# Late bank, early tokens, a gate product in column groups: an edit in four places of a two-block transformer kernel

## The chip, the cores and the metric

The kernel runs on one core of one Trainium2 chip. The metric is the device time of one execution in microseconds, the median of several runs. TensorE does the matmuls, VectorE, ScalarE and GpSimd the rest, and SyncE (SP) issues nearly all loads.

## The reference, cut to what matters

Two transformer blocks of two layers each run over 256 tokens of width 1024, all float32.

```python
for l in range(2):                         # first block
    mod = silu(c) @ w_ada[l] + b_ada[l]    # 6 vectors of 1024: sh1, sc1, g1, sh2, sc2, g2
    h = layer_norm(x) * (1 + sc1) + sh1
    x = layer_norm(ALPHA * x + g1 * mixer(h, w_in[l], ...), ln1[l])   # projections, rope, attention
    h = layer_norm(x) * (1 + sc2) + sh2
    x = layer_norm(ALPHA * x + g2 * moe(h), ln2[l])      # 16 experts of width 256, 2 of them per token
# second block
h = x @ w_in; q, k, v, r, lr = split(h)    # lr has 16 columns
log_a = log_sigmoid(lr @ w_gate2 + b_gate) / 16          # 16 -> 512
# ... gated linear attention, then experts of width 512, then differential attention, experts again
```

There are four expert stages, moe0 to moe3. In each of them a token goes to two of 16 experts; the weights of all 16 are read.

## The kernel before

**The stream.** All large weights come from memory as a stream of 212 slots of 2 MB (128 x 4096), in the order of use. A slot lands in one of several banks of on-chip memory: ring 0 to 3, and up to five more that are open only in some spans of the stream (`OPEN`): two banks at the end of `area` (`RING`, `RING + 1`), one in the constants `cst` (`RING + 2`), one more in `area`, one in `early`. `ring_order` deals out the banks ahead of time: each slot takes the open bank that was given out longest ago, and a bank that has just opened comes first. SP issues the loads strictly in the order of the slots (L1504). Ahead of each load it waits until the slot that last lay in that bank has been used, and ahead of the first load into a bank that has just opened it waits for what lay there: in the expert stages for the last sums of the output projection before them (`acc_filled`). A slot that waits holds back all behind it. Behind slot `kvq` SP issues 16 small loads of the relative bias (`load_rel_bias`, L1490), which wait for the last slot that lay in bank `RING + 1`.

The names of slots: `ada_first` (4 pieces of w_ada), `in0`, `pa0`, `out0`, `moe0` (24 slots), the same for layer 1, `gla_in` (6), `gla_out` (2), `moe2` (48), `v`, `kvq`, `kvq_rest`, `v_rest`, `diff_out`, `moe3` (48).

**The start.** SP issues three small tables, slot 0, slot 1, the tokens X, slot 2, and then the rest. TensorE multiplies each of the four first pieces of w_ada by silu(c) in column groups (`ada_parts`, L904: partial sums in four groups of 32 columns, kept apart), ScalarE copies them out (`ada_take`), and TensorE sums the groups and the partitions by a product with ones (`ada_finish`, L925). ScalarE then makes `mod_col`. VectorE norms the tokens (L2069, L2088), TensorE flips them (`flip_tokens`, L588), and ScalarE writes the flipped and scaled tokens to `HT` (`take_tile`, L1556), for which it needs all four pieces. Then the products with w_in start (L549, L566).

**Other pieces of w_ada.** 20 more are weighed and summed over k by VectorE or GpSimd (`ada`) during the mixer. TensorE sums them over the partitions (`ada_sums`). For gains the result is wanted on all partitions: a product with ones in f32 (L921), and a product of a one-hot column with the table of biases (L922). Two pieces of each layer, 10 and 11 (`ADA_LATE`), are summed in `ada_late`, in the expert stage, right ahead of the counts.

**The expert stages.** VectorE ranks the scores and writes `chosen_h` (L2289). TensorE counts with it each token's place in its expert's queue (L693 to L696). From this VectorE makes `SEL` (`select`, L2383), the matrices that gather the tokens. The tokens are split into a high part `X_HI` and a low part `X_LO` in float32r; ScalarE writes the high parts, GpSimd the low part of the first tile (L510) and VectorE that of the second (`low_part`, L2262). TensorE gathers both parts of both tiles (`gather`, L706), ScalarE and VectorE scale the result to `XG`, and then eight pairs of experts follow: `up` (L749), the activation, `down` (L801), and the scatter to the tokens (L783). `residual_norm` ends the stage.

**The gate of the second block.** TensorE makes lr, transposed, by eight matmuls of 16 columns (`flipped` with n=16), as the input tile `HT` of the second token tile comes from ScalarE. ScalarE copies it to `LRT` (16 rows). For each token tile one product with w_gate2 (16 rows, L1212) and one with the bias (1 row, L1213) follow. While VectorE and ScalarE make the log decay, TensorE works on the next slot (L566).

Of the kernel before, what the change touches and what calls it, by code (L numbers as in the profile page):

```python
# [71 lines left out]
ADA_SPLIT = [4, 5]  # L72

# [46 lines left out]
for _name, _n in (("ada0", W), ("ada1", W), ("gate2", W), ("b_gate", W), ("rel", DH)):  # L120
    ROWS[_name] = (N_ROWS, _n)
    N_ROWS += _n
# [62 lines left out]
def nth(j):  # L185
    return j // 4 + 1
# [4 lines left out]
                   (SLOTS["moe2"] + 4, SLOTS["v"]), (SLOTS["moe3"] + 4, N_SLOTS)),  # L191
# [45 lines left out]
def build(nc, x, consts, vecs, cols, rows, ln_vecs, stream, rel_rows, out):  # L237
    with ExitStack() as ctx:
# [53 lines left out]
        X, XN, MT, HT = tiles(x_sb, TT), tiles(xn_sb, TT), tiles(mt_sb, KD), tiles(ht_sb, KD)  # L292
        GAIN, LNV = gain_sb.rearrange("p (a b) -> p a b", a=2), tiles(ln_sb, 2)
# [70 lines left out]
        LRT = area[0:LR, 11264:11264 + T]  # L364
# [95 lines left out]
        def _(pool):  # L460
# [25 lines left out]
            def ada(l, i):  # L486
# [15 lines left out]
                pool.tensor_tensor(a, w[:, 0:W], w[:, W:2 * W], ALU.add).then_inc(ada_by_pool, 1)  # L502
                n_done[0] += 1
                pool.wait_ge(ada_by_pool, n_done[0])
# [26 lines left out]
        def _(pe):  # L531
# [150 lines left out]
            def moe(number, fc):  # L682
# [17 lines left out]
                def gather(double, kk, bank):  # L700

                    pe.wait_ge(sel_ready, 4 * number + double + 1)
                    for k in range(2):
                        c = (2 * kk + k) * P
                        for n, (x_part, t) in enumerate((x_part, t) for x_part in (X_HI, X_LO) for t in range(TT)):
                            ins = pe.matmul(bank[:, k * 4 * CAP:(k + 1) * 4 * CAP], x_part[:, t, c:c + P],  # L706
                                            SEL[:, t, double * 4 * CAP:(double + 1) * 4 * CAP], start=n == 0, stop=n == 3)
                    ins.then_inc(gathered, 1)

                pe.wait_ge(x_lo_ready, TT * (number + 1))  # L710
# [200 lines left out]
            def ada_sums(l, n, bank, filled):  # L911
# [2149 lines left out]
```

## Time and profile before

| | |
|---|---|
| median of 3 runs | 1560.81 us (1560.26 to 1561.62) |
| the profiled execution's own time | 1562.76 us |
| its span, from the first to the last instruction | 1561.0 us |
| mean granted clock of TensorE | 0.966 of full speed |
| TensorE busy | 1453.3 us, 93% of the span |
| VectorE, ScalarE, GpSimd busy | 549.8, 342.2 and 124.5 us |
| moved by DMA | 462 MB, mean 296 GB/s |

The shares are averages over stages with different limits. Matmuls overlap, and their records are modelled, so that a busy share of 93% does not say that TensorE sets the end everywhere. The DMA engines are full in some stages and nearly idle in others. The stage in which an edit lies decides what it is worth.

### The profile page before, as it was taken

How to read it: one execution, taken by the hardware profiler on the slowest of the kernel's cores; microseconds unless marked ns; L12 is line 12 of the kernel's file. 1: busy time of each engine (PE TensorE's matmuls, PEld its weight loads, DVE VectorE, ACT ScalarE, POOL GpSimd, SP SyncE). 2: the span in 40 equal slices, each digit the busy share in tenths (PEclk: the TensorE clock that was granted, in tenths of full speed). 3: DMA queues.
4: the chain of work that ended last, by engine and by line, in shares of the span. 5: the costliest groups of instructions: out<-in, count | busy, mean ns of one | idle time of the engine just before them, and what ended most of it. 6: DMA issues, size and time to landing. Idle time of an engine off the chain costs nothing.

```text
span 1561.0 us, 16280 instructions
## 1 busy us (share of the span) xinstructions
PE 1453.3 (93%) x6800; PEld 831.0 (53%) x6800; DVE 549.8 (35%) x1073; ACT 342.2 (22%) x779; POOL 124.5 (8%) x60
## 2 busy tenths in 40 slices
PE   5999999899799999899989998999988998999985
PEld 2686885454378788445436444434335764444432
DVE  2582235523566124543251133121004353211113
ACT  2213331311211323132132132101002343111101
POOL 0007620000001900000000000000000000000000
PEclk8999999799899999989999998999999999999998
DMA  9985352899657632399946717999999421999995
GB/s 373 424 340 225 155 216 108 349 392 424 262 222 279 280 139 78 128 393 396 425 166 220 265 54 302 429 425 429 427 427 400 168 102 70 428 428 428 427 429 214
DMA packets 36459, 462.36 MB, mean 296 GB/s; under 512 B 4008, under 2 KB 6328, under 8 KB 8056
## 3 DMA queue, kind: packets, MB, share of 16 engines
q1 hardware_dynamic: 33824, 448.91, 70.1%
q0 software_dynamic: 1520, 10.19, 1.6%
q10 hardware_dynamic: 1032, 2.10, 0.7%
q8 instruction: 58, 0.95, 0.2%
q14 instruction: 25, 0.20, 0.0%
HBM read 458.04 MB, written 3.15 MB: 295 GB/s over the span
## 4 chain that ended last, share of the span: by engine, by line
PE 83%; DMA 10%; DVE 4%; ACT 2%; issue 1%; SPq 0%; DVEq 0%; ACTq 0%
PE work L749 17%; PE work L566 13%; PE work L801 9%; PE work L549 8%; PE acc L566 7%; DMA ring<-in_stream 5%; PE acc L549 5%; PE work L706 5%; DMA early<-in_stream 4%; PE acc L783 3%; PE work L558 3%; PE work L1240 2%; PE acc L1384 2%; PE work L1035 1%; PE acc L1057 1%
## 5 line engine op out<-in xcount | busy, mean ns | idle before, releaser
L749 PE MATMUL work<-ring,area 128*64 128x512 f32 x896 | 200.4, 594 | 8.8 <-DMA ring<-in_stream 8.8
L749 PEld LDWEIGHTS work<-ring,area 128*64 128x64 f32 x896 | 64.0, 137 | 134.7 <-issue 119.4
L566 PE MATMUL work<-ht_sb,ring 128*128 128x256 f32 x576 | 128.8, 384 | 0.0
L566 PEld LDWEIGHTS work<-ht_sb,ring 128*128 128x128 f32 x576 | 110.1, 192 | 16.9 <-issue 2.2
L2432 DVE SCALAR_TENSOR_TENSOR area<-area,comb_slot,work 128x256 f32<-128x256 f32 (+1 forms) x32 | 19.7, 614 | 273.4 <-ACT area L1652 273.4
L566 PE MATMUL acc<-ht_sb,ring 128*128 128x256 f32 x512 | 114.1, 382 | 0.0
L566 PEld LDWEIGHTS acc<-ht_sb,ring 128*128 128x128 f32 x512 | 96.3, 190 | 14.6 <-issue 2.0
L2452 DVE TENSOR_TENSOR area_r<-work,area_r 128x512 fp32r<-128x512 f32 x64 | 44.3, 692 | 137.6 <-ACT area_r L1663 109.3
L749 PE MATMUL work<-area 128*64 128x512 f32 x384 | 86.7, 593 | 2.5 <-DMA area<-in_stream 2.5
L801 PE MATMUL work<-ring,area 128*64 128x512 f32 x384 | 86.6, 596 | 0.0
L1652 ACT ACTIVATE area<-work 128x256 f32<-128x256 f32 (+1 forms) x32 | 15.7, 491 | 316.3 <-PE work L749 316.3
L549 PE MATMUL work<-ring,ht_sb 128*128 128x512 f32 (+1 forms) x192 | 79.3, 575 | 5.1 <-ACT ht_sb L1556 2.6
L1532 ACT ACTIVATE area<-work 128x512 f32<-128x512 f32 (+2 forms) x54 | 31.2, 587 | 239.5 <-PE work L566 121.2
L783 PE MATMUL acc<-area_r,mt_sb_r 128*128 128x512 f32 x256 | 73.6, 410 | 3.3 <-DVE area_r L2452 3.3
L549 PE MATMUL acc<-ring,mt_sb 128*128 128x512 f32 x160 | 71.4, 596 | 2.6 <-DVE mt_sb L2670 2.6
L706 PE MATMUL work<-ht_sb_r,area_r 128*128 128x256 f32 x256 | 59.1, 315 | 5.9 <-DVE ht_sb_r L2383 5.9
L494 POOL TENSOR_TENSOR ring<-ring,silu_c 128x4096 f32<-128x4096 f32 x7 | 49.1, 7015 | 168.2 <-DMA ring<-in_stream 168.2
L549 PEld LDWEIGHTS work<-ring,ht_sb 128*128 128x128 f32 x192 | 39.4, 208 | 42.5 <-issue 35.8
L801 PE MATMUL work<-area 128*64 128x512 f32 x256 | 58.4, 598 | 0.0
L749 PEld LDWEIGHTS work<-area 128*64 128x64 f32 x384 | 28.1, 137 | 56.7 <-issue 51.9
L706 PEld LDWEIGHTS work<-ht_sb_r,area_r 128*128 128x128 f32 x256 | 44.4, 214 | 25.6 <-issue 19.5
L469 POOL DMA_DIRECT2D ln_sb<-in_ln_vecs x8 | 4.4, 556 | 664.7 <-DVE x_sb L2112 498.3
(344 smaller groups left out, 1952.3 us busy)
## 6 DMA issues: line engine op xcount, KB each, us to landing
ring<-in_stream SPq DMA_DIRECT2D x138, 2048.0 KB, 12.2
area<-in_stream SPq DMA_DIRECT2D x46, 2048.0 KB, 12.2
cst<-in_stream SPq DMA_DIRECT2D x14, 2048.0 KB, 17.4
early<-in_stream SPq DMA_DIRECT2D x14, 2048.0 KB, 22.9
ln_sb<-in_ln_vecs POOLq DMA_DIRECT2D x8, 1024.0 KB, 12.2
rel_rows<-mt_sb ACTq DMA_DIRECT2D x1, 2048.0 KB
cst<-in_consts POOLq DMA_DIRECT2D x1, 1209.0 KB, 16.2
x_sb<-in_x SPq DMA_DIRECT2D x1, 1024.0 KB, 15.6
```

Of the source, the lines that this page charges most:

```text
L494: pool.tensor_tensor(by_k, by_k, silu_c[:, :, None].to_broadcast([P, KD, W]), ALU.mult).then_inc(pool_chain, 1)
L549: ins = pe.matmul(dst, src[:, k, t * P:(t + 1) * P], w[:, k, c0:c0 + n], start=k == 0, stop=k == KD - 1)
L558: ins = pe.matmul(dst, tokens[:, k, r, :], w[:, k, c0:c0 + n], start=k == 0, stop=k == KD - 1)
L566: ins = pe.matmul(dst, w[:, k, c0:c0 + n], src[:, k0 + k, :], start=k == 0, stop=k == ks - 1)
L706: ins = pe.matmul(bank[:, k * 4 * CAP:(k + 1) * 4 * CAP], x_part[:, t, c:c + P], SEL[:, t, double * 4 * CAP:(double + 1) * 4 * CAP], start ...
L749: ins = pe.matmul(banks[half][e * CAP:(e + 1) * CAP, :], tokens[:, k, at:at + CAP], w[:, kk, e, half * W:(half + 1) * W], start=k == 0, st ...
L783: ins = pe.matmul(acc[2 * n + t][:, :], BACK[:, p, t * P:(t + 1) * P], part[:, n, :], start=p == 0 and part is Y_HI, stop=p == PAIRS - 1 a ...
L801: ins = pe.matmul(banks[n][e * CAP:(e + 1) * CAP, :], ACTT[:, f * P + e * CAP:f * P + (e + 1) * CAP], w[:, i, e, n * W:(n + 1) * W], start ...
L1240: ins = pe.matmul(bank[:, :], HT[:, k, t * P:(t + 1) * P], w[:, k, :], start=k == 0, stop=k == KD - 1)
L1384: ins = pe.matmul(acc[2 * n + t][:, :], MT[:, k, t * P:(t + 1) * P], w[:, k, :], start=k == 0, stop=k == KD - 1)
L1532: act.activation(dst, src, func, scale=scale).then_inc(bank_drained[j % 4], 1)
L2452: dve.tensor_tensor(Y_LO[:, n, :], banks[n][:, :], Y_HI[:, n, :], ALU.subtract).then_inc(y_lo_ready, 1)
```

## The change

- The bank `RING + 1` opens at the eighth slot of moe2 and of moe3 (`+ 7`) and no longer at the fifth (`+ 4`).
- The tokens X are loaded ahead of slot 1, and TensorE and ScalarE take them ahead of the second finish and the third piece.
- The late pieces 10 and 11 get their bias from GpSimd, on one row of the sum, and are split into a high and a low part in float32r; TensorE sums both parts by two products with ones. For this the table of biases is in another order, and one more row is loaded.
- VectorE does `low_part` behind `select(0)` and no longer ahead of the count's use. The first gather does six matmuls and waits for the second tile's low part only then.
- lr is made in four column groups, copied out by four copies to rows 0, 32, 64 and 96 of a `LRT` of 128 rows, which VectorE has set to 1 before. The table `gate2` holds the bias as its row 16 and is loaded three times more (without the bias) for the other groups, so that one product of 128 rows sums the groups and adds the bias.

```diff
-                   (SLOTS["moe2"] + 4, SLOTS["v"]), (SLOTS["moe3"] + 4, N_SLOTS)),
+                   (SLOTS["moe2"] + 7, SLOTS["v"]), (SLOTS["moe3"] + 7, N_SLOTS)),
...
-            for i, n in enumerate(ADA_SPLIT):
-                at = 32 * (i + 1)
+            for at, n in ((32, ADA_SPLIT[0]), (64, ADA_SPLIT[1]), (96, ADA_LATE[1])):
                 pool.dma_start(early[at:at + 1, 0:DEPTH * W], rows[n:n + 1, 0:DEPTH * W]).then_inc(rows_loaded, 16)
+            o, again = ROWS["gate2"][0], ROWS["gate2_again"][0]
+            for g in range(32, P, 32):
+                pool.dma_start(early[g:g + 32, o:o + W], rows[:, again:again + W]).then_inc(rows_loaded, 16)
...
+                if late:
+                    i = ADA_LATE.index(piece)
+                    row_at = slice(96 * i, 96 * i + 1)
+                    pool.wait_ge(rows_loaded, 16 * 7)
+                    pool.tensor_tensor(a[row_at, :], a[row_at, :], early[row_at, layer * W:(layer + 1) * W], ALU.add)\
+                        .then_inc(pool_chain, 1)
...
+                    pool.tensor_copy(LATE_HI[:, i, :], a).then_inc(pool_chain, 1)
...
+                    pool.tensor_tensor(ada_lo[:, (n % 2) * W:(n % 2 + 1) * W], a, LATE_HI[:, i, :], ALU.subtract).then_inc(ada_by_pool, 1)
...
+                    first = double == 0 and kk == 0
+                    if first:
+                        steps = [(k, n) for k in range(2) for n in range(3)] + [(k, 3) for k in range(2)]
+                    for i, (k, n) in enumerate(steps):
+                        if first and i == 6:
+                            pe.wait_ge(x_lo_ready, TT * (number + 1))
...
-                pe.wait_ge(x_lo_ready, TT * (number + 1))
+                pe.wait_ge(x_hi_ready, TT * (number + 1))
+                pe.wait_ge(x_lo_ready, TT * number + 1)
...
-                if l and n in ADA_SPLIT:
+                if l and n in ADA_SPLIT or n in ADA_LATE:
                     lo = ada_lo[:, ((ada_done[0] - 1) % 2) * W:((ada_done[0] - 1) % 2 + 1) * W]
-                    pe.matmul(bank[:, :], ones_r[:, :], ada_hi[:, :], start=True, stop=False)
+                    hi = LATE_HI[:, ADA_LATE.index(n), :] if n in ADA_LATE else ada_hi[:, :]
+                    pe.matmul(bank[:, :], ones_r[:, :], hi, start=True, stop=False)
                     ins = pe.matmul(bank[:, :], ones_r[:, :], lo, start=False, stop=True)
...
             ada_finish(*ADA_FIRST[0], parts_0)
-            parts_2 = ada_parts(s + 2)
-            ada_finish(*ADA_FIRST[1], parts_1)
             pe.wait_ge(inputs_loaded, 16 * N_INPUTS)
             for t in range(TT):
                 flip_tokens(t, FIRST_BANKS[t])
                 await_tokens()
+            parts_2 = ada_parts(s + 2)
+            ada_finish(*ADA_FIRST[1], parts_1)
...
-            flipped(bank[0:LR, 0:T], HT, column("lr"), 0, filled, n=LR)
+            for k in range(KD):
+                part_transposed(k)
+                g = 32 * (k % 4)
+                ins = pe.matmul(bank[g:g + LR, 0:T], column("lr")[:, k, :], HT[:, k, :], start=k < 4, stop=k >= 4)
+            ins.then_inc(filled, 1)
...
-                pe.matmul(bank[:, :], LRT[:, t * P:(t + 1) * P], rows_("gate2", LR), start=True, stop=False)
-                pe.matmul(bank[:, :], ones[0:1, :], rows_("b_gate", 1), start=False, stop=True).then_inc(filled, 1)
+                o = ROWS["gate2"][0]
+                pe.matmul(bank[:, :], LRT[:, t * P:(t + 1) * P], early[:, o:o + W], start=True, stop=True).then_inc(filled, 1)
...
+            sp.dma_start(X, x.rearrange("(t p) d -> p t d", p=P)).then_inc(inputs_loaded, 16)
             sp.dma_start(slot(1)[:, :], stream[1, :, :]).then_inc(slot_loaded[RING_BANK[1]], 16)
-            sp.dma_start(X, x.rearrange("(t p) d -> p t d", p=P)).then_inc(inputs_loaded, 16)
...
             ada_take(s, 0)
-            ada_take(s + 1, 1)
-            ada_finish(*ADA_FIRST[0])
             act.wait_ge(inputs_loaded, 16 * N_INPUTS)
             for t in range(TT):
                 norm_root(t)
+            ada_take(s + 1, 1)
+            ada_finish(*ADA_FIRST[0])
...
+            for g in range(0, P, 32):
+                ins = act.activation(LRT[g:g + LR, :], work[j % 4][g:g + LR, 0:T], ACT.Copy)
+            ins.then_inc(bank_drained[j % 4], 1)
...
                 select(0)
+                low_part(number)
...
+                    residual_norm(None, "columns", lambda: dve.memset(LRT, 1.0))
```

## Rows read from the trace of the kernel before

**Rows 1.** The chain that ended last, in order of time: start us, us, what.
```profile
38.48 22.58 PE work L549 x64
...
289.71 6.55 PE work L706 x32
...
955.88 6.29 PE work L706 x32
...
1495.39 35.57 DMA early<-in_stream
```

**Rows 2.** Stretches: length; busy us (count) by engine; PEclk, DMA share, GB/s.
```profile
911.00:946.00 35.00, 33.83 (x110) 15.87 (x108) 6.79 (x16) 8.93 (x17) 2.34 (x1) 1.00 0.07 29
...
966.00:1162.00 196.00, 187.35 (x922) 78.48 (x920) 29.27 (x45) 22.84 (x40) 0.56 (x1) 1.00 1.01 428
...
831.00:847.00 16.00, 16.00 (x66) 13.63 (x67) 5.66 (x9) 4.41 (x5) 0.00 (x0) 0.89 0.91 387
```

**Rows 3.** Single loads of SP: moe2+4 (946.4) and moe2+8 (965.8), issue to landing.
```profile
L1504 SPq DMA_DIRECT2D area<-in_stream x1: 328/328/328, 946.4 to 946.4; - x1
...
DMA to landing us min/median/max: 7.7/7.7/7.7
...
L1504 SPq DMA_DIRECT2D ring<-in_stream x1: 328/328/328, 965.8 to 965.8; - x1
...
DMA to landing us min/median/max: 9.1/9.1/9.1
```

**Rows 4.** The bias loads on SP (ns min/median/max, first to last start); TensorE at kvq_rest.
```profile
L1490 SPq DMA_DIRECT2D area<-rel_rows x16: 331/432/12928, 1157.8 to 1179.3; - x16
...
1214.87 7.17 PE L566 MATMUL work<-ht_sb,cst 128*128 128x256 f32 x32
```

**Rows 5.** Instructions in order of time, moe2: start us, us, engine, line, what, [idle].
```profile
953.68 1.22 DVE L2262 TENSOR_TENSOR xn_sb_r<-xn_sb,area_r 128x1024 fp32r<-128x1024 f32 x1
953.70 0.21 PE L693 MATMUL work<-chosen_h,before_h 128*128 128x32 bf16 x1 [3.06 <-DVE chosen_h L2289]
```

**Rows 6.** Instructions in order of time, moe0, ahead of the gather.
```profile
280.39 2.06 PE L921 MATMUL acc<-early,ones 128*128 128x512 f32 x2
...
286.73 0.19 DVE L2289 SCALAR_TENSOR_TENSOR chosen_h<-route 128x32 bf16<-128x32 f32 x1
...
288.39 0.21 PE L693 MATMUL work<-chosen_h,before_h 128*128 128x32 bf16 x1
```

**Rows 7.** Instructions in order of time, the start.
```profile
18.72 1.29 DVE L2069 BATCH_NORM_STATS2 stat<-x_sb 128x6 f32<-128x512 f32 x2 [6.53 <-DMA x_sb<-in_x]
...
23.64 3.64 PE L904 MATMUL acc<-ring,cst 128*32 128x512 f32 x16 [4.54 <-DMA ring<-in_stream]
...
28.94 1.95 PE L588 MATMUL work<-cst,xn_sb 128*128 128x128 f32 x8
...
32.52 1.92 PE L904 MATMUL acc<-ring,cst 128*32 128x512 f32 x16
```

**Rows 8.** The load of w_in's third block, and TensorE where it takes it.
```profile
L1504 SPq DMA_DIRECT2D ring<-in_stream x1: 328/328/328, 54.2 to 54.2; - x1
...
DMA to landing us min/median/max: 12.1/12.1/12.1
...
69.80 14.08 PE L566 MATMUL work<-ht_sb,ring 128*128 128x256 f32 x64
```

**Rows 9.** Instructions in order of time, the gate of the second block.
```profile
815.69 2.90 ACT L1556 ACTIVATE ht_sb<-acc,col 128x128 f32<-128x128 f32 x8 [8.97 <-PE acc L588]
816.64 3.61 PE L566 MATMUL work<-ht_sb,col 128*16 128x256 f32 x16 [0.55 <-ACT ht_sb L1556]
...
827.25 1.12 PE L1212 MATMUL work<-early,area 16*128 16x512 f32 x2
...
830.88 15.77 PE L566 MATMUL work<-ht_sb,ring 128*128 128x256 f32 x64
...
839.33 1.22 DVE L2711 TENSOR_TENSOR area<-area,early 128x1024 f32<-128x1024 f32 x1 [3.65 <-ACT early L1925]
```

More of the change, by code:

```diff
@@ L72 @@
 ADA_SPLIT = [4, 5]
+ADA_ROWS = [ADA_LATE[0], *range(1, ADA_LATE[0]), 0, *range(ADA_LATE[0] + 1, ADA_SLOTS)]
 SLOTS = {}
@@ L119 @@
 N_ROWS = 0
-for _name, _n in (("ada0", W), ("ada1", W), ("gate2", W), ("b_gate", W), ("rel", DH)):
+for _name, _n in (("ada0", W), ("ada1", W), ("gate2", W), ("gate2_again", W), ("rel", DH)):
     ROWS[_name] = (N_ROWS, _n)
@@ L702, in gather @@
                     pe.wait_ge(sel_ready, 4 * number + double + 1)
-                    for k in range(2):
+                    parts = [(x_part, t) for x_part in (X_HI, X_LO) for t in range(TT)]
+                    steps = [(k, n) for k in range(2) for n in range(4)]
+                    first = double == 0 and kk == 0
[4 more added lines that the diff above has]
+                            pe.wait_ge(x_lo_ready, TT * (number + 1))
+                        x_part, t = parts[n]
                         c = (2 * kk + k) * P
-                        for n, (x_part, t) in enumerate((x_part, t) for x_part in (X_HI, X_LO) for t in range(TT)):
-                            ins = pe.matmul(bank[:, k * 4 * CAP:(k + 1) * 4 * CAP], x_part[:, t, c:c + P],
-                                            SEL[:, t, double * 4 * CAP:(double + 1) * 4 * CAP], start=n == 0, stop=n == 3)
+                        ins = pe.matmul(bank[:, k * 4 * CAP:(k + 1) * 4 * CAP], x_part[:, t, c:c + P],
+                                        SEL[:, t, double * 4 * CAP:(double + 1) * 4 * CAP], start=n == 0 and not (first and k), stop=n == 3 and (k == 1 or not first))
                     ins.then_inc(gathered, 1)
-                pe.wait_ge(x_lo_ready, TT * (number + 1))
+                pe.wait_ge(x_hi_ready, TT * (number + 1))
+                pe.wait_ge(x_lo_ready, TT * number + 1)
                 for kk in range(KD // 2):
@@ L2141, in residual_norm @@
                         take_root(t)
+                        if t and before_last is not None:
+                            before_last()
                         normalised(t)
@@ L2675, in _ @@
                 route_first(l)
-                low_part(l)
                 experts(l, F_1 // P, scale, shift, lambda: None, combine_first)
-                residual_norm(None, "norm" if l < DEPTH - 1 else "columns")
+                if l < DEPTH - 1:
+                    residual_norm(None, "norm")
+                else:
+                    residual_norm(None, "columns", lambda: dve.memset(LRT, 1.0))
             for t in range(TT):
@@ L2774, in _ @@
             route_second(0)
-            low_part(2)
             rows = [lambda: row_norm(0), lambda: row_norm(1)]
@@ L3037 @@
     rows = np.zeros((32, N_ROWS), a["b_ada"].dtype)
-    for name, m in (("ada0", a["b_ada"][0].reshape(ADA_SLOTS, W)), ("ada1", a["b_ada"][1].reshape(ADA_SLOTS, W)),
-                    ("gate2", a["a_w_gate2_2"][0]), ("b_gate", a["a_b_gate_2"]), ("rel", a["rel_table_2"])):
+    for name, m in (*((f"ada{l}", a["b_ada"][l].reshape(ADA_SLOTS, W)[ADA_ROWS]) for l in range(DEPTH)),
+                    ("gate2", np.concatenate([a["a_w_gate2_2"][0], a["a_b_gate_2"].reshape(1, W)])),
+                    ("gate2_again", a["a_w_gate2_2"][0]), ("rel", a["rel_table_2"])):
         o, n = ROWS[name]
```

29 lines of the change are left out of this document (20 added, 9 removed).

## The prediction, made before the result was known

> **What bounds the kernel now.** I read the chain of work first. It alternates: from the start to about 1090 us it is TensorE nearly throughout, and then, in each of the two large expert stages, it ends in a DMA piece of some 30 to 35 us (two in each stage, one stands in [rows 1]). The stage windows say why: from 966 to 1162 us the DMA engines are busy all the time at 428 GB/s, so a slot of 2.1 MB costs 4.9 us, six slots make an expert pair, 29.4 us, and TensorE needs some 25 us for the pair. Just before, from 911 to 946 us, the same engines are 7% busy [rows 2]. So up to the third expert stage a microsecond saved on TensorE is a microsecond of the end. In the third and the fourth only the moment counts at which the stream of slots begins to run without a gap. The reader is to see these two regimes; each edit belongs to one of them.
>
> **The stream of the third and fourth expert stage (bank of area three slots later).** SP issues slots in order. The slot moe2+4 goes to area's bank and waits for the last sum of gla_out, at 946.4 us; the three behind it, whose banks come free earlier, wait with it. The first of the four, issued to an idle queue, lands after 7.7 us [rows 3]; the fourth three slots later, about 969. The next one, moe2+8, is issued at 965.8, when TensorE frees the bank of moe2+0, and lands after 9.1 us [rows 3]: 1.4 us of that is the queue in front of it. With the change moe2+4 to +6 take banks that gla_in and gla_out give back before or at that sum, and moe2+7 alone waits for it. Three slots more don't help as such: the bank of moe2+8 still has to be freed by TensorE. But the queue in front of it is gone, so it lands 7.7 us after its issue: 1.4 us gained, and from then on the stream is tied to TensorE's first release and no longer to 946.4. The fourth stage shows the same pair of rows (9.1 us for the slot issued at 1338.1). Term: 1.4 twice, 2.8 us. Below, nothing is lost, since no slot waits for more than it did; above, the term can't pass 1.4, since the release is TensorE's.
>
> The order of banks also changes which slot the relative bias waits for: now moe2+44, afterwards moe2+47, the last, freed some 15 us later (three slots). SP issues the 16 loads from 1157.8 to 1179.3, one of them for 12.9 us behind a full queue, the others 0.43 us apart [rows 4]. Issued from about 1172.8 behind two slots only, 16 x 0.45 further they are out, at about 1180.2: up to 1 us later, for SP and the four slots behind them. TensorE needs the first of those at 1214.9 [rows 4], so nothing is counted.
>
> **Selection ahead of the low part.** In the third stage TensorE makes the counts at 953.70, and VectorE spends 1.22 us from 953.68 on the low part before it takes them [rows 5]; the gather starts at 955.88 [rows 1]. In the first stage there is no such hold: counts at 288.39 [rows 6], gather at 289.71 [rows 1], 1.32 us. So the third would start at 953.70+1.32, 0.86 us earlier. The low part then ends 1.2 us after the selection; the six matmuls that the gather can do without it take 6 x 0.2 = 1.2 us (32 in 6.29 us, [rows 1]), so the new wait costs between nothing and 0.2; I take nothing. If the six ran at full clock it would be 0.5. The stream starts from TensorE's release, so this goes into the end once the queue is gone: 0.9 twice, 1.7 us. Without the first edit only about 0.6 of each would.
>
> **Late rows in two parts.** In the first stage TensorE works on them from 280.39 (each x2 group about 2 us, four of them) until 288.39, though VectorE had chosen by 286.73+0.19 [rows 6]. Four float32r matmuls of one part each instead of eight f32 records end before 284 even at the slowest rate of these rows, so the counts follow the choice at about 287.0: 1.4 us. The low part no longer lies under TensorE's work but under the gather, as above. The second layer's rows give 1.2. Term 2.6 us, all on TensorE's path. GpSimd pays three more operations on 128x512 and one row for each of four pieces, ahead of the release of the piece's slot. It idles for tens of microseconds between its last piece and the low part; the sums are wanted behind that, and the slots that it frees later are reloaded behind other waits of SP. Zero; without that cover TensorE would wait at the counts. The bound above is 2.2 us more, if VectorE also speeds up, which nothing suggests; below, the row for the clock in the rivals.
>
> **Start.** Slot 0, slot 1 and X land one after another; X arrives at 18.72 [rows 7]. In the other order X is there a slot's time (4.9) earlier, 13.8, and slot 1 at 18.7. VectorE's norm is then done before TensorE is free. TensorE afterwards: parts of slot 1 from 18.7, 3.6 us at half clock (the row at 23.64) or 1.9 (the row at 32.52); finish 1.0 to 1.8; 16 transposes, 3.6 us at half clock (28.94 to 32.52), 2 at full; parts of slot 2, 1.9; finish 1; parts of slot 3 (landed 4.9 behind slot 2, 28.5), 1.9. With the clock rising during the transposes that ends at about 31; it ends at 34.4 now. So 3.4 us. All at full clock 4.0; all at half it would end at 36.8, a loss of 2.4. Then a cap: the third block of w_in lands at 54.2+12.1 = 66.3, in a saturated queue that doesn't move with TensorE, and TensorE wants it at 69.8 [rows 8]. The four new small row loads (0.2 MB, 0.5 us) come in front of it: 66.8. More than 3.0 us can't be kept. Term 3.0, bounds 3.5 and -2.4. SP's other loads keep their order.
>
> **Gate in column groups.** The eight lr matmuls (16 columns of 128, 256 wide) take from 816.64 until the next row at 820.18, 3.5 us. ScalarE makes their input from 815.69 for 2.90 us, to 818.6 [rows 9]. In column groups they are faster than their input, end some 0.5 us behind it, 819.1: 1.1 us. The Trainium skill, TensorEngine Tiling (Array Packing), section Theoretical Speedup, gives up to four times for 32 columns or fewer; by it alone the term would be 2.7 and the time 1.6 us lower, and here ScalarE's row stands against it. The two gate2 products are four groups now, 827.25 to 830.88; two remain at 0.9: 1.8 us. What follows takes 15.77 us for 64 records at a mean granted clock of 0.89 [rows 2, 9], where the same 64 take 14.08 in [rows 8]: 1.7 us at 1.2 instead of 2.4 GHz, right behind matmuls that fill 16 rows and 1 row of the array. With 128 rows I expect that the clock stays: 1.7. ScalarE's four copies for one lie under 7.1 us of TensorE work. The new end of TensorE's block, 842.0, must find the log decay ready: VectorE finishes it at 840.55 [rows 9], and it moves 1.1 earlier too, 2.5 us of cover. VectorE's memset lies where TensorE is still at the first tile. Term 4.6, between 1.2 (clock falls anyway, in the ScalarE-paced part as well) and 6.2.
>
> **Sum.** 2.8 + 1.7 + 2.6 + 3.0 + 4.6 = 14.7 us off the profiled execution's own 1562.76 (span 1561.0 and 1.8 around it): 1548.1. That execution is 1.95 above the median of the runs, 1560.81, so the median becomes 1546.2.
>
> **Rivals.** (a) The stream does not follow TensorE: some slot behind moe2+8 is short, and stages three and four give only 1.2 of their 4.5. For: with no queue in front, TensorE's next releases are only a few microseconds ahead of the stream. Against: each slot waits for the same slot eight back as now. 1549.5. (b) The start gives nothing, because TensorE now idles until 18.7 and the clock is low longer: 1549.2, at worst 1551.6. For: [rows 7] shows 3.64 against 1.92 for the same work, and when the clock rises decides. (c) The clock in the first two expert stages: TensorE, busy for 8 us now, is idle for some 5 before the gather. If the low clock then reached through it and the first 16 matmuls behind it (3.6 at full, 7.2 at half) that costs some 3.6 each, and the time would be 1553.4. Against: its 32 matmuls take 6.55 us [rows 1], 0.2 each, so the clock is low there already, in spite of the 8 us of work. The Trainium skill, TensorE: Matmul & The Clock Gate, section on HAM oscillation, has the rule that idle gaps throw the clock back to half; by that rule the trace agrees that gaps cost, and it is this rival. (d) The clock falls in the gate stage: 1.7 to 3.4 less, 1548 to 1549.6. (e) The other side: the 16 loads of the relative bias, now behind the last slot, meet a full queue as one did for 12.9 us, and everything behind them on SP is late. Their followers would be issued at about 1193 and land near 1202; TensorE waits from 1214.9 on. It decides only from 13 us more on, and the kernel is slower only if it takes another 15: a loss of some 3 at a delay of 30, 1564. (f) The change does nothing: the gains at the start and in the first stages are swallowed by a stream that has its own pace. Against: no DMA piece in the chain between 36 and 1090 us. 1560.8.
>
> **How the numbers follow.** Forecast 0.60; (a) 0.10, (b) 0.10, (c) 0.07, (d) 0.08, (e) 0.02, (f) 0.03. Predicted 1546.2, by itself 1544 to 1549 with the clock's phases. The range goes to 1542 below (4.6 to 6.2, 3.0 to 3.5, clock better in each gather) and to 1552 above, which takes in (a), (b) and (d) and leaves out (c), (e), (f). A measurement of this kernel tells 0.2%, 3.1 us, from no change: faster 0.95, same 0.03, slower 0.02.
>
> **What would show it.** Parts of slot 3 end near 31, and the first block of w_in starts near 35.5. Gathers start some 1.3 us behind the choice in all four stages. No low clock in the block behind gate2. The slots moe2+8 and moe3+8 land 7.7 us after issue, with idle DMA right before, and the last slot lands 14 to 15 us earlier than now. Wrong it would be if the gap between the last landing and the end grew, or if TensorE waited for a slot before 90 us.

## The result, and the profile after

The changed kernel takes 1552.42 us (median of 5 runs, 1550.71 to 1554.29), beside 1561.52 us for the kernel before (5 runs, 1560.26 to 1563.01): ratio 0.9943, 95% interval 0.9928 to 0.9957. A second job gave 1552.45 and 0.9944 (0.9928 to 0.996). So it is faster by some 9 us (0.6%), where 14.7 were predicted, and 1552.4 lies just outside the range of 1542 to 1552. Five executions of the experiments ran in a slow state (1591 to 8380 us), and the medians and ratios below leave them out.

The span of the profiled execution fell from 1561.0 to 1552.5 us. The chain that ended last shows at once where it went wrong, in the first 90 us (start us, us, what):

```profile
34.13 15.71 PE work L570 x32
...
49.86 19.07 DMA ring<-in_stream
...
68.97 15.77 PE work L587 x64
```

The first block of w_in starts at 34.13 instead of 38.48 [rows 1]: 4.35 us were gained there, more than the 3.0 of the term. But in the middle of w_in stands a piece that the chain before does not have: TensorE waits for slot 9, the third block. SP's loads one by one show this slot (issued 49.9), and the two slots of the third expert stage, moe2+8 (958.8) and moe2+9 (962.3):

```profile
L1538 SPq DMA_DIRECT2D ring<-in_stream x1: 328/328/328, 49.9 to 49.9; - x1
...
DMA to landing us min/median/max: 19.1/19.1/19.1
...
L1538 SPq DMA_DIRECT2D ring<-in_stream x1: 328/328/328, 958.8 to 958.8; - x1
...
DMA to landing us min/median/max: 7.7/7.7/7.7
...
L1538 SPq DMA_DIRECT2D area<-in_stream x1: 327/327/327, 962.3 to 962.3; - x1
...
DMA to landing us min/median/max: 10.0/10.0/10.0
```

Slot 9 was issued 4.3 us earlier than in [rows 8] and needed 7 us longer: it lands at 68.9 instead of 66.3. TensorE lost 3.4 us in waiting, and then 1.7 more, because the 64 matmuls behind the wait take 15.77 us where [rows 8] has 14.08. The slot moe2+8 lands 7.7 us after its issue, as predicted (9.1 in [rows 3]). The row of the next slot, which I had not read before, is this one of the kernel before (issued 969.2):

```profile
L1504 SPq DMA_DIRECT2D area<-in_stream x1: 328/328/328, 969.2 to 969.2; - x1
...
DMA to landing us min/median/max: 10.4/10.4/10.4
```

It takes 10.4 before and 10.0 after. In three profiles of the kernel before it takes 10.3 to 10.6, in eleven with the bank at +7 and other edits 9.8 to 10.7, mean 10.2. From the second slot on, the edit of the bank gives 0.2 to 0.4 us and not 1.4.

The windows of the changed kernel that answer to [rows 2] (length; busy us by engine; PEclk, DMA share, GB/s), and the start:

```profile
30.00:46.00 16.00, 13.81 (x44) 7.11 (x41) 4.05 (x6) 8.85 (x29) 4.10 (x9) 0.89 1.01 343
905.00:940.00 35.00, 33.84 (x110) 15.88 (x108) 6.79 (x16) 8.93 (x17) 2.35 (x1) 1.00 0.40 148
958.00:1150.00 192.00, 185.04 (x912) 77.80 (x908) 29.26 (x45) 22.85 (x40) 0.56 (x1) 1.00 1.00 422
```

The idle queue ahead of the third expert stage is now used (148 GB/s instead of 29), and the stage behind it is full as before. At the start, from 30 to 46 us, the engines are just as full as in the kernel before (share 1.00), but move only 343 GB/s instead of 382. TensorE in order of time, at the gate of the second block:

```profile
815.40 2.61 PE L1240 MATMUL work<-ht_sb,col 128*16 128x256 f32 x16 [0.55 <-ACT ht_sb L1590]
817.94 7.13 PE L570 MATMUL work<-ring,ht_sb 128*128 128x512 f32 x16
824.91 1.88 PE L1247 MATMUL work<-early,area 128*128 128x512 f32 x4
826.63 13.98 PE L587 MATMUL work<-ht_sb,ring 128*128 128x256 f32 x64
```

Against [rows 9]: lr to the next row 2.54 us (3.54 before), the gate products 1.72 (3.63), the block behind them 13.98 (15.77). And in the third expert stage:

```profile
942.89 1.14 PE L681 MATMUL work<-ht_sb,route_w 128*32 128x128 f32 x16 [1.12 <-ACT ht_sb L1621]
...
948.10 0.21 PE L714 MATMUL work<-chosen_h,before_h 128*128 128x32 bf16 x1 [3.05 <-DVE chosen_h L2330]
...
949.26 1.22 DVE L2303 TENSOR_TENSOR xn_sb_r<-xn_sb,area_r 128x1024 fp32r<-128x1024 f32 x1
...
949.49 0.77 PE L734 MATMUL work<-ht_sb_r,area_r 128*128 128x256 f32 x2 [1.12 <-DVE ht_sb_r L2424]
```

The counts are at 948.10 and the gather starts 1.39 us later (2.18 in [rows 5] and [rows 1]); the low part ends under the gather.

The same moments in three traces, us from the start, with the difference to the kernel before. The last column is the first experiment below.

| moment | before | changed | copies late |
|---|---|---|---|
| SP issues in0+11 | 92.50 | 93.35 (+0.85) | 89.47 (-3.03) |
| SP issues moe0+10 | 318.35 | 317.71 (-0.64) | 313.00 (-5.35) |
| SP issues moe1+14 | 725.84 | 724.45 (-1.39) | 719.02 (-6.82) |
| SP issues gla_out+0 | 851.64 | 845.60 (-6.04) | 840.05 (-11.59) |
| moe2+9 lands | 979.64 | 972.29 (-7.35) | 966.93 (-12.71) |
| SP issues moe3+1 | 1230.04 | 1222.25 (-7.79) | 1216.75 (-13.29) |
| the last slot lands | 1540.71 | 1532.25 (-8.46) | 1526.53 (-14.18) |

So the changed kernel loses 0.85 us at the start, gains 1.5 in the first expert stage, 0.7 in the second, 4.6 at the gate, 1.3 at the third stage, 0.4 between the two and 0.7 in the fourth; the terms were 3.0, 1.4, 1.2, 4.6, 2.3, nothing and 2.3. All differences of this table are against one profile of the kernel before, whose start was slower than that of its two others (experiment 5).

### The profile page after: what moved, and what is told of

It is laid out like the page before. It is cut to its first block, busy times and chain, and to the rows that moved or that the text cites. A ratio compares the mean times of both kernels' runs of the same rounds, so it can differ in the third digit from the quotient of the medians.

```text
span 1552.5 us, 16286 instructions
## 1 busy us (share of the span) xinstructions
PE 1436.9 (93%) x6788; PEld 826.5 (53%) x6788; DVE 549.3 (35%) x1074; ACT 343.1 (22%) x782; POOL 138.3 (9%) x76
## 4 chain that ended last, share of the span: by engine, by line
PE 80%; DMA 11%; DVE 5%; ACT 2%; issue 1%; SPq 0%; DVEq 0%
PE work L778 17%; PE work L587 12%; PE work L830 9%; PE work L570 7%; PE acc L587 7%; DMA ring<-in_stream 7%; PE acc L570 5%; PE work L734 5%; DMA early<-in_stream 4%; PE acc L812 3%; PE work L579 3%; PE work L1274 2%; PE acc L1418 2%; PE work L1065 1%; DVE stat L2107 1%
## 5 line engine op out<-in xcount | busy, mean ns | idle before, releaser
L778 PEld LDWEIGHTS work<-ring,area 128*64 128x64 f32 x896 | 64.3, 137 | 133.8 <-issue 119.0
L1566 ACT ACTIVATE area<-work 128x512 f32<-128x512 f32 (+1 forms) x53 | 30.8, 591 | 239.1 <-PE work L587 122.1
L778 PEld LDWEIGHTS work<-area 128*64 128x64 f32 x384 | 27.7, 137 | 57.1 <-issue 52.7
```

What stands on the lines that cost most here:

```text
L778: ins = pe.matmul(banks[half][e * CAP:(e + 1) * CAP, :], tokens[:, k, at:at + CAP], w[:, kk, e, half * W:(half + 1) * W], start=k == 0, st ...
L1566: act.activation(dst, src, func, scale=scale).then_inc(bank_drained[j % 4], 1)
```

## The experiments

There were eighteen more runs, of thirteen variants and of the two kernels again. Gains below are one minus the ratio, times 1561.5 us, the median of the kernel before over all jobs. For slot 9, the third block of w_in, the landing in the profiled execution is given. "Undone" means that the changed kernel, or a variant of it, has this one edit taken back.

**1. The three copies of gate2 behind slot 11** (changed kernel otherwise; two jobs).

```diff
-            o, again = ROWS["gate2"][0], ROWS["gate2_again"][0]
-            for g in range(32, P, 32):
-                pool.dma_start(early[g:g + 32, o:o + W], rows[:, again:again + W]).then_inc(rows_loaded, 16)
             pool.wait_ge(slot_loaded[RING_BANK[5]], 16 * nth_round(5))
...
             load_ln(0)
+            pool.wait_ge(rows_loaded, 16 * 4)
+            pool.wait_ge(slot_loaded[RING_BANK[11]], 16 * nth_round(11))
+            o, again = ROWS["gate2"][0], ROWS["gate2_again"][0]
+            for g in range(32, P, 32):
+                pool.dma_start(early[g:g + 32, o:o + W], rows[:, again:again + W]).then_inc(rows_loaded, 16)
```

The gate product waits for the copies, and the earlier users of the small rows no longer do (not shown).

> The changed kernel, with the three copies of the gate2 rows loaded behind the landing of slot 11 instead of ahead of the tables, and the gate products waiting for them. Theory (small rows): the three extra loads of 64 KB and their many small descriptors took 2 to 2.7 us of the queue ahead of slot 9; without them slot 9 (third block of w_in) lands at about 66.5 to 67 us instead of 68.9, TensorE waits under 1.5 us for it instead of 3.4, the clock does not fall behind the wait, and the time is 2.5 to 4.3 us lower than that of the changed kernel (1552.4), so 1548 to 1550. Rival (order): slot 9 is late because the slots' places in the queue moved with TensorE's earlier releases; it still lands at 68.5 or later, and the time stays within 0.7 us of 1552.4.

> The copies behind slot 11 a second time. Small rows: slot 9 lands at 66 to 66.7 again, and slot 15 is issued 3 us earlier than in the kernel before (92.5); the median is 1549 to 1551. If the first profile was an accident, slot 9 lands at 67.5 or later.

> The changed kernel as it is, a second time, to see how much of its start repeats. If the late third block of w_in belongs to the kernel, slot 9 lands at 68.5 or later again and TensorE waits 3 us for it; the median is 1552.4 within 1. If it was an accident of one execution, slot 9 lands near 66.5 and the profiled time is 1550 or lower.

Measured: 1551.10 us, ratio 0.9934 (0.9921 to 0.9947), and 1549.73 us, 0.9923 (0.991 to 0.9935); the ten runs have a median of 1550.0, the eleven of the changed kernel 1552.4. Slot 9 lands at 66.2 and 66.1, against 68.9 and 68.0 in the two profiles of the changed kernel. Chain, load of slot 9 and window of the first run:

```profile
34.70 23.33 PE work L572 x64
...
66.84 14.01 PE work L589 x64
```

```profile
L1542 SPq DMA_DIRECT2D ring<-in_stream x1: 328/328/328, 51.2 to 51.2; - x1
...
DMA to landing us min/median/max: 15.1/15.1/15.1
```

```profile
30.00:46.00 16.00, 13.84 (x45) 6.89 (x38) 5.29 (x8) 8.88 (x29) 3.24 (x7) 0.79 1.01 392
```

No wait is left in w_in, the 64 matmuls take 14.01 us, and in the same 16 us the full queue moves 392 GB/s instead of 343 (in the second profiles 385 and 353), which is 6.27 MB instead of 5.49. The 0.78 MB that are missing with the copies are 1.8 us at 428 GB/s; the copies themselves are 0.20 MB. So the copies made slot 9 late, and that belongs to the kernel, not to one execution. The first median, 1551.1, lies above the 1548 to 1550 that I expected, the second inside its range.

**2. The price of the copies** (changed kernel): loaded twice, or in one load of 96 rows.

```diff
+            for g in range(32, P, 32):
+                pool.dma_start(early[g:g + 32, again:again + W], rows[:, again:again + W]).then_inc(rows_loaded, 16)
```

```diff
-            for g in range(32, P, 32):
-                pool.dma_start(early[g:g + 32, o:o + W], rows[:, again:again + W]).then_inc(rows_loaded, 16)
+            pool.dma_start(early[32:P, o:o + W], bass.AP(rows.tensor, again, [[0, 3], [N_ROWS, 32], [1, W]])).then_inc(rows_loaded, 16)
```

> The changed kernel with the three copies loaded twice, the second time into columns that nothing reads. Small rows: 96 more rows of 2 KB ahead of slot 9 cost it another 1.5 to 3 us, so it lands at 70 to 72 and the time is 1.5 to 3 us above the changed kernel (1552.4): 1554 to 1555.5. By bytes alone 0.2 MB are 0.5 us: slot 9 within 0.5 us of the changed kernel's 68 to 69, time 1553.

> The changed kernel with the three copies in one load of 96 rows, at the same place. If the rows (packets) cost, nothing changes: slot 9 at 68 to 69, 1552.4 within 1. If each load costs by itself, two thirds of the 1.8 to 2.7 us go: slot 9 at about 66.8 to 67.2 and 1550.5 to 1551.

Measured: twice 1554.25 us, ratio 0.9957 (0.9945 to 0.997), slot 9 at 71.0; one load 1550.69 us, 0.9941 (0.9928 to 0.9954), slot 9 at 68.6. By the ratios neither is clear of the changed kernel's interval; what decides is slot 9. The two loads of slot 9, in this order:

```profile
L1540 SPq DMA_DIRECT2D ring<-in_stream x1: 328/328/328, 53.3 to 53.3; - x1
...
DMA to landing us min/median/max: 17.7/17.7/17.7
```

```profile
L1537 SPq DMA_DIRECT2D ring<-in_stream x1: 328/328/328, 52.0 to 52.0; - x1
...
DMA to landing us min/median/max: 16.5/16.5/16.5
```

Slot 9 lands at 66.1 to 66.7 in seven other profiles that have no early copies (the norm rows at their old place), at 67.6 to 69.5 in four with three of them, and at 71.0 with six. So a set costs 2.2 to 2.5 us of the full queue, five times what its bytes would. That one load instead of three helps is not shown: the median is the one that the rival had (1550.5 to 1551), but slot 9 is where it was, and the ratio is within the interval of the changed kernel.

Where the 2.3 us go can be read in the DMA queues from 20 to 70 us, of the changed kernel and then of copies_late (packets, MB, share of the 16 engines; q1 has the stream, q0 the loads that GpSimd issues):

```profile
q1 hardware_dynamic: 1156, 16.84, 84.6%
q0 software_dynamic: 640, 3.05, 15.8%
...
q1 hardware_dynamic: 1225, 17.79, 85.8%
q0 software_dynamic: 544, 2.85, 14.5%
```

The copies' own 0.20 MB take 1.3% of the 50 us, 0.65 us. The stream takes 2.51 us for each MB instead of 2.41, which is 1.7 us for its 16.84 MB. Most of the price is thus that the stream's own packets are slower beside the copies. In the nine profiles without early copies the stream takes 2.40 to 2.43 us for each MB, in the four with three copies 2.48 to 2.51, with one load of 96 rows 2.51, and with six copies 2.54. That it is the small rows that do it is argued and not shown: no run changed the size of the rows and kept the bytes, or loaded the same rows to other partitions.

The Trainium skill, DMA: Bandwidth & Descriptors, section Rules for kernel authors, says of many small transfers to coalesce them and that below 64 KB one pays mostly overhead. The trace agrees that such loads, just at 64 KB each, cost more than their bytes (2.3 us for 0.46), but not on the remedy: the one load was still of 96 rows of 2 KB, and slot 9 stayed at 68.6. Moving them out of the full stretch was what helped.

**3. The norm rows behind slot 11 as well** (`load_ln(0)` moved behind the copies; two jobs).

> As copies_late, and the 1 MB load of the norm's rows (ln_sb) is moved behind the landing of slot 11 as well. Both theories allow it to bring slot 9 forward: 1 MB at 420 GB/s is 2.5 us, so slot 9 at about 64.5 to 65, ahead of the moment at which TensorE wants it (65.6). Small rows: 0.5 to 1 us less than copies_late, because the rest of TensorE's wait goes. Rival (order): 2.5 us less than copies_late, because the whole wait is still there to be removed.

> The version with copies and norm rows behind slot 11 a second time, as the yardstick of the run beside it: 1549.4 within 0.7; slot 9 lands at 64 to 64.6, before TensorE wants it.

Measured: 1549.42 us, ratio 0.9924 (0.9911 to 0.9937), slot 9 at 64.2; and 1548.73 us, 0.9926 (0.9913 to 0.9938), slot 9 at 64.3. The ten runs have a median of 1549.3, which is the best version, 3.1 us below the changed kernel. Slot 9 comes 2.0 us earlier than in experiment 1 by a load of 1 MB in rows of 8 KB, which would be 2.5 us by its bytes at 428 GB/s: this load cost no more than its bytes, unlike the copies.

**4. The start's order**: alone on the kernel before, undone in the changed kernel, and undone in the version of 3. The edit is that of the diff (SP, TensorE, ScalarE).

> The kernel before with the tokens loaded ahead of slot 1 and transposed ahead of its parts, nothing else. Small rows: without the copies slot 9 lands at 66.2 as before, TensorE reaches it at about 65.7, and everything behind is 3.0 to 3.5 us earlier; 1557.5 to 1558.5. Rival (order): slot 9 lands at 68 or later here too, and the time is within 1 us of the kernel before.

> The changed kernel with SP's, TensorE's and ScalarE's order at the start as in the kernel before (slot 1 ahead of the tokens). Small rows: TensorE reaches the third block of w_in at 69.8 again, slot 9 lands at 68 to 69.5, so TensorE hardly waits and stands at slot 14 where the kernel before did, within 0.5 us: time 0.5 to 1 us lower than the changed kernel. Rival (the start's edit is worth its 3 us, and something else took it away): time about 3 us above the changed kernel, 1555.5.

> The version with copies and norm rows behind slot 11, with the start in the order of the kernel before. It prices the start's order where no load holds it up. Theory (half of the 3.0 was the clock of the one profiled execution): with the clock up early the first block of w_in starts at 35.8 instead of 34.5, 1.3 us lost; with it low at 38.5, 4 us lost; median 1.3 to 2.5 above 1549.4. Prediction: 3.0 to 3.5 above.

Measured: alone 1560.38 us, ratio 0.9989 (0.998 to 0.9998), a gain of 1.7 us (0.3 to 3.1), slot 9 at 66.2; undone in the changed kernel 1551.36 us, 0.9936 (0.9923 to 0.9949), no worse than with it; undone in the version of 3 1551.17 us, 0.9934 (0.9922 to 0.9947), against 0.9925 with it: 1.4 us, which is not clear of the noise by itself. So the order is worth some 1.5 us, and not the 3.0 to 3.5 that I still expected of it alone, and nothing where slot 9 is held back by the copies.

**5. The kernel before, two more profiled executions.**

> The kernel before, unchanged, a second profiled execution. If the start has forms by the phase of the clock, the first block of w_in starts anywhere from 35.7 to 38.5 us, with a finish of x8 matmuls near 1.0 or 1.8 us ahead of it; if the start is fixed, at 38.5 within 0.3.

> The same a third time: 35.7 to 38.5 by the clock's phase, or 38.5 within 0.3 if the start is fixed.

Measured: 1559.97 and 1561.41 us. The chain of the first, in order of time:

```profile
23.36 3.32 PE acc L904 x16
26.68 0.98 PE acc L925 x8
27.66 0.93 PE work L588 x8
...
35.36 22.57 PE work L549 x64
```

And of the second:

```profile
23.59 3.64 PE acc L904 x16
27.24 1.21 PE acc L925 x8
28.44 0.93 PE work L588 x8
...
36.13 23.45 PE work L549 x64
```

The same instructions reach the first block of w_in at 35.4 and 36.1 us, where the profile of the prediction has 38.48 [rows 1]. In that one the chain has for the eight transposes

```profile
29.08 1.81 PE work L588 x8
```

(1.95 with their overlap in [rows 7]), here 0.93: the granted clock was at 0.50, which is 1.2 GHz, until 32.6 us there, and until 26.2 and 27.7 us here, where the transposes have 2.4. In eight profiles with the old order the block starts at 35.4 to 38.5, mean 36.8; in twelve with the new order at 34.1 to 36.7, mean 35.5. The forecast had been made against the slowest of them.

**6. The bank**: alone on the kernel before, undone in the changed kernel, and undone in the version of 3. The diff shows the edit undone; alone it is its reverse.

```diff
-                   (SLOTS["moe2"] + 7, SLOTS["v"]), (SLOTS["moe3"] + 7, N_SLOTS)),
+                   (SLOTS["moe2"] + 4, SLOTS["v"]), (SLOTS["moe3"] + 4, N_SLOTS)),
```

> The kernel before with area's bank joining at moe2+7 and moe3+7, nothing else. Theory (second slot of an idle queue is late too): the slot moe2+8 lands 1.4 us earlier and moe2+9 only 0.4, likewise in the fourth stage; 0.4 to 0.8 us below the kernel before, 1560.6 to 1561. Prediction's term: 2.8 us below, 1558.6.

> The changed kernel with area's bank joining the ring at moe2+4 and moe3+4 again. Theory (start of an idle queue costs its second slot too, which lands 5.8 us behind the first instead of 4.7): the edit was worth 0.4 us and the 0.9 of the selection in the third stage, and 0.1 and 0.4 in the fourth, so 1.5 to 2 us above the changed kernel. Rival (the prediction's term of 1.4 in each stage, lost elsewhere): 3 to 4 us above. Rival (nothing): within 0.5.

> The version with copies and norm rows behind slot 11, with area's bank at moe2+4 and moe3+4 again. It repeats bank_at_4 on a quieter start. Theory (second slot late too, and the selection's 0.9 and 0.4 locked without the bank): 1.5 to 2.3 us above 1549.4. Rival (3.5, as the medians of bank_at_4 gave): 1552.9.

Measured: alone 1559.95 us, ratio 0.9992 (0.9983 to 1.0), a gain of 1.2 us (0 to 2.7). Its trace does not have the 7.7 us of the prediction. The slots moe2+8 and moe3+8 are issued to a queue that moved nothing for 6 and 5 us, and take

```profile
L1504 SPq DMA_DIRECT2D ring<-in_stream x1: 328/328/328, 963.5 to 963.5; - x1
...
DMA to landing us min/median/max: 8.7/8.7/8.7
```

and 9.0 us. In the eleven profiles with the bank at +7 and other edits both take 7.5 to 7.9. Why they don't here stays open, but for the stream it makes no difference: moe2+9 lands 4.7 us behind moe2+8 here and 5.8 in the changed kernel, so in both 13.4 to 13.5 us behind the issue of moe2+8, for 13.8 in the kernel before.

Undone in the changed kernel 1555.92 us, 0.9965 (0.9953 to 0.9977), a loss of 3.4 us; undone in the version of 3 1553.42 us, 0.9952 (0.994 to 0.9964), a loss of 4.2. My theory (1.5 to 2.3) missed this; the rival with the prediction's term was nearer. The load of moe2+8 in bank_at_4:

```profile
L1538 SPq DMA_DIRECT2D ring<-in_stream x1: 328/328/328, 960.0 to 960.0; - x1
...
DMA to landing us min/median/max: 10.2/10.2/10.2
```

With the bank at +4 the slot is issued 5.8 us earlier than in the kernel before and lands 4.8 earlier: it takes 10.2 us instead of 9.1, since the queue ahead of it still starts from area's bank. What TensorE gains in these stages is then lost in the queue, and the bank's edit sets it free. Between the trace of late_loads_bank_at_4 and that of late_loads_again the difference grows by 3.3 us from the gate to the end. About 0.9 of it is in the third stage, 1.0 in the fourth, and 1.4 between them, in a stage that the bank does not touch. The two stages alone give the 1.9 that my theory had. Between them the 16 matmuls behind the norm take

```profile
1177.88 9.73 PE work L570 x16
```

in bank_at_4 and 9.68 in late_loads_bank_at_4, but 8.85 in the changed kernel and 8.73 in the kernel before. The granted clock rises 5.2 us into this row in bank_at_4 and 3.5 us into it in the changed kernel. The bank is not what sets it: the row takes 9.58 in gate_alone (bank at +4, as in the kernel before), 10.06 in late_loads_low_part_first (bank at +7), and 8.6 to 9.0 in the other sixteen profiles. What does stays open, and with it how much of the 3.4 and 4.2 us is the bank's.

**7. The gate in column groups alone**, on the kernel before, its copies behind slot 11.

> The kernel before with the gate stage in column groups, its copies loaded behind slot 11, nothing else. Prediction's term: 4.6 us between the last sum of the second expert stage and the first block behind the gate (lr 1.1, gate2 1.8, clock 1.7), which the stream of the third stage takes over whole: 1561.5 - 4.6 = 1556.9. Rival: part of it is swallowed where the stream starts behind area's bank; then under 3.5 us at slot moe2+9.

Measured: 1556.87 us, ratio 0.9973 (0.9962 to 0.9983), a gain of 4.2 us. TensorE's rows:

```profile
814.86 2.62 PE L1215 MATMUL work<-ht_sb,col 128*16 128x256 f32 x16 [0.55 <-ACT ht_sb L1567]
817.40 7.13 PE L554 MATMUL work<-ring,ht_sb 128*128 128x512 f32 x16
824.38 1.88 PE L1224 MATMUL work<-early,area 128*128 128x512 f32 x4
826.09 13.98 PE L571 MATMUL work<-ht_sb,ring 128*128 128x256 f32 x64
```

Each of the three parts is as in the changed kernel. SP issues gla_in+0 1.8 us and gla_out+0 6.6 us earlier than in the kernel before, 4.8 in between. The stream of the third stage took over 4.7 of it (moe2+9 lands at 973.17, 6.5 earlier), so the rival of a swallowed part falls.

**8. Late rows and selection alone**, on the kernel before, and the low part first again in the version of 3.

> The kernel before with the late rows in two parts and the selection ahead of the low part in all four stages, nothing else (one more row of 4 KB is loaded at the start). Prediction's terms: 1.4 and 1.2 us in the first two stages, and, with the bank at moe2+4 as before, 0.6 in each of the others. Theory now: 1.4 to 2.3 in the first, 0.7 to 0.9 in the second by the phase of the clock, and nothing in the other two, because there the slots wait in a queue that starts from area's bank, not from TensorE's release: slot moe2+9 gains under 0.2 behind moe2+4. 1558.4 to 1559.4.

> The version with copies and norm rows behind slot 11, with the low part ahead of the selection and the gather in one piece as in the kernel before; bank, rows, gate and start stay. Prediction's terms: 0.9 in the third and the fourth stage each and 0.5 to 1.2 in the first two: 2.5 to 4 us above 1549.4. Theory now: 0.9 in the third, 0.4 to 0.9 in the fourth by the phase of the clock, 1 in each of the first two; 2.5 to 3.5 above.

Measured: alone 1557.19 us, ratio 0.9976 (0.9967 to 0.9985), a gain of 3.8 us, more than the 2.1 to 3.1 that I expected; low part first 1551.3 us, 0.9939 (0.9924 to 0.9955), a loss of 2.2 against 0.9925, which is not clear of the noise. By the trace of the first the gain is 2.3 us in the first stage, 0.6 in the mixer behind it, 0.9 in the second stage and nothing in the third and fourth, where moe2+9 lands 4.1 us earlier than before, the same 4.1 with which the second stage had ended. In the version with the low part first, the third stage still frees its first bank 0.9 us earlier against the last sum of gla_out (954.24 less 935.81 there, 958.84 less 940.37 in the changed kernel, 965.80 less 946.41 in the kernel before: 18.4, 18.5 and 19.4), so the edit is not what sets it. Against the trace of late_loads_again this one loses 3.3 us from the slot in0+11 to the end: 0.8 in the first two stages, 1.0 in the fourth, and 1.6 between the third and the fourth, where the edit has no part; there stands the row of 10.06 us of experiment 6.

## Why the prediction was wrong

**The start is the step that failed, at two places of its working.** The term said: "The four new small row loads (0.2 MB, 0.5 us) come in front of it: 66.8. More than 3.0 us can't be kept." The cap was the right thing to look at, and its slot the right one, but the loads were priced by their bytes. Slot 9 came at 68.9, 68.0, 69.5 and 67.6, and with the copies out of the way at 66.2, 0.1 from the cap without them. This cost some 2.4 us in the medians. That the trace with the copies late shows the 3.0 to the tenth (row in0+11 of the table) is luck: its repetition has 2.61, and before_again_1 is at that slot 3.12 earlier with no edit at all. The other place is the sum itself. The 3.4 us of the start were counted down from a block start at 38.48, and then "that execution is 1.95 above the median" was taken off again. But the late clock of [rows 7] was itself a part of these 1.95: five of eight profiles with this order don't have it. What the order saves in the mean of eight and twelve profiles is 1.3 us, and 1.4 to 1.7 by the ratios. In effect the result is the rival (b), "the start gives nothing", but its reason was another: TensorE's idle time until 18.7 did not cost it, the copies did.

**The bank: its size was read from one slot of one profile.** In the changed kernel moe2+8 and moe3+8 land 7.7 us after their issue, as said; with the bank's edit alone they take 8.7 and 9.0, also behind an idle queue (experiment 6). And what the first slot gains the second gives back: moe2+5 in the kernel before landed 5.5 us behind moe2+4, and moe2+9 now lands 5.8 behind moe2+8, where 4.9 is the pace; where the first took 8.7, it was 4.7. The gain was 0.2 to 0.4 in the stream of the third stage and no more in the fourth; alone, the edit gave 1.2 (0 to 2.7) of the 2.8. That it is worth 3.4 to 4.2 when taken out of the changed kernel is in part what the prediction said of the pair ("Without the first edit only about 0.6 of each would"), and in part the open point of experiment 6.

**Selection: right at its own row, wrong in its effect.** The gather follows the choice after 1.4 us, as in the first stage. But the 16 logit matmuls ahead of it now run partly at the low clock (1.14 us at 942.89 for 0.91, the granted clock 0.54 from 943 to 944), and the two behind them take 0.62 for 0.40, so that the choice itself comes 0.44 later against the last sum (7.73 us from 940.37 to 948.10, before 7.29 from 946.41 to 953.70). The gather starts 0.35 earlier, not 0.86. The 0.9 at TensorE's first release is there all the same, as the gather takes 5.73 us for 32 instead of 6.29, and that came without the edit too (experiments 7 and 8). Over the four stages the edit gives 2.2 by the ratios, which the noise and the open row of experiment 6 make uncertain.

**Late rows** gave 1.5 and 0.7 in the changed kernel, and 2.3 and 0.9 without the other edits, for 1.4 and 1.2; what the selection does in these two stages is in these numbers. Here too the remainder is the clock in the gather, 6.41 us for 32 in the changed kernel and 5.56 with the copies late. Rival (c), the low clock through the gather and the 16 matmuls behind it, did not come: those 16 take 3.65 us. GpSimd's additional work cost nothing that the table shows.

**The gate** was right in all three parts: 1.0, 1.9 and 1.8 us for 1.1, 1.8 and 1.7, together 4.6 to 4.8; rival (d) falls. By the Trainium skill, TensorEngine Tiling (Array Packing), section Theoretical Speedup, which the prediction set beside it, up to 1.6 us more could have come, an estimate; the trace is with ScalarE's row: lr takes 2.54 us and ends 0.6 behind its input (2.90 us from 814.45).

**The relative bias** (rival (e)) did no harm. The slots behind it are issued 0.8 us later against the end of the third stage, and nothing waits for them. (The prediction's 1180.2 should be 1180.0 by its own terms.)

Of the signs that were named, these held: the block start before 35.5, the gather 1.3 to 1.4 us behind the choice, the full clock behind gate2, and 7.7 us for the two slots. Two did not: the last slot lands 8.5 us earlier and not 14 to 15, and TensorE waited for a slot before 90 us, which was the sign of a wrong prediction.

**The accounts.** Gains by ratio, each edit alone on the kernel before: gate 4.2, rows and selection 3.8, start 1.7, bank 1.2; together 10.9. The changed kernel with late copies gains 10.3 and 12.0 in its two jobs, so the sum closes. The changed kernel gains 8.9 and 8.7; the early copies are the 2.3 between. The terms of the same four were 4.6, 2.6 + 1.2, 3.0 and 2.8. Of the 14.7, with 1.7 for the selection, 3.8 are missing in the four terms, the bank (1.6) and the start (1.3) first, and 2.3 by the copies: 6.1, for 5.8 missing in the changed kernel. The forecast of 1546.2 was also counted from a median of 1560.81 for the kernel before, which was 1561.52 in the job of the result; that is 0.7 of its 6.2.

## What to carry to other kernels

Don't price small loads in a full queue by their bytes alone: here 0.20 MB in rows of 2 KB cost five times their bytes, and 1 MB in rows of 8 KB no more than its bytes. Put everything that isn't wanted soon behind the last transfer that something waits for. Before an edit is counted down from a profiled execution, ask whether the stretch it starts from is typical: where its rows sit at the low clock, a part of the gain may be one that other executions have already, and it must not be subtracted twice. When a queue is to start idle, read its second and third transfer as well as the first, and in more than one profile.

## What the runs showed of the hardware

- 96 rows of 2 KB (0.20 MB), loaded beside a full stream of 2 MB slots, took 2.3 us of it on average, 0.65 by themselves and the rest because the stream took 2.51 us for each MB instead of 2.41. The DMA engines' share stayed at 1.01 while the rate fell from 392 to 343 GB/s. A full share does not mean the full rate.
- The same program reached its first large block at 35.4, 36.1 and 38.5 us in three executions, by when the clock rose to 2.4 GHz (26.2, 27.7 and 32.6 us); the difference stayed to the end (the last slot lands 2.8, 1.4 and 0 us earlier). TensorE had been busy at the low clock since 23.4 to 23.6 us in all three.
- A slot issued to an idle queue (moe2+8 and moe3+8 with the bank at +7) lands after 7.5 to 7.9 us in eleven profiles and after 8.7 and 9.0 us in one. The next slot lands 13.2 to 14.2 us behind the issue of the first in all twelve, and the others follow 4.9 apart.
